# Block attention's TensorE steps: run after every 24 weight matmuls, two quarter tiles' worth together, instead of after every 12

## The chip, the cores and the metric

The kernel runs on one core of a Trainium2 chip. The metric is the device time of one execution in microseconds (us). TensorE (PE in the profile) does the matmuls, and the loading of its stationary operand is shown apart as PEld; VectorE is DVE, ScalarE is ACT, GpSimd is POOL, SyncE is SP.

## The reference, cut to what matters

One inference step of a two-layer decoder trunk, for a prompt of 256 tokens and 8 samples of 8 tokens (320 tokens in all, model width 2048, everything in float32). Layer 0 is a Mamba-2 / short-convolution mixer, layer 1 is block-sparse attention ("MoBA"); each is followed by a cross-attention into 256 memory tokens. The change touches layer 1 alone:

```
q, k, v, g = split(h @ w_in)                   # 2048 -> 5120 columns: 40 column tiles of 128
prompt:  s = q @ k.T + alibi; softmax; o = p @ v          # 16 heads, 4 KV heads, 256 tokens
sample:  kmean = mean of each 256-key block of the cache (8 blocks of 256 past keys, paged)
         the 3 blocks with the highest q . kmean are kept, and the own block of 8 new tokens
         s = q @ k_sel.T + alibi; softmax; o = p @ v_sel
out = (o * silu(g)) @ w_out                    # 2048 -> 2048: 16 column tiles
```

## The kernel before

All projections go through one stream of weight tiles of 2048x128 (1 MB each). SP loads tile n into one of 4 buffers (`Trunk.load`), ACT rounds it to float32r (`Trunk.high`, L123, 1.9 us), DVE makes the remainder (`Trunk.low`, L128, 2.3 us), and TensorE multiplies it in 48 matmuls of 128x320 (`Proj.parts`: 32 with the high half, L167, then 16 with the low half, L172). The results of successive tiles alternate between two banks of PSUM; DVE takes each one out (`evacuate`).

The attention is woven into the 40 tiles of the layer's input projection. Each tile is cut into 4 quarters of 12 weight matmuls (`weave`, L1670). Quarter qr = 4j + qi is quarter qi of tile j, and behind its 12 matmuls TensorE runs the attention steps that `Moba.steps(qr)` lists (L2169). The two loops of `scalar_program` and `vector_program` go over the same quarters in the same order, and do their halves of the same steps; all engines are tied by semaphores alone, each engine's queue strictly in order.

The samples are worked off in 8 units U (2 samples and 8 heads each), one unit per period of 12 quarters (3 tiles), starting at quarter 40. With x for the quarter inside a period (x = (qr - 40) mod 12), a period holds:

- **K** at x = 0, 3, 6, 9 (called K0 to K3 below): 16 transposes of key pages (L2315) into four fills of a ring of three PSUM banks. ACT copies each fill out to `past_keys` (L2424, x4), and a fill waits until the fill three before it in the ring has been copied (`turn_bank`, L2290).
- **S** at x = 2, 5, 8, 11: scores (L2334), with the own block at x = 11 (L2336). DVE takes them in (`scored`: L2607, L2608, L2611) and, for all but a few early ones, also waits for the T step of the same quarter.
- **T** at x = 5, 8, 11 and 2 of the next period: transposes of probabilities (L2343, L2345), one fill each, copied by ACT (L2430).
- **V** at x = 8, 11 and 2, 5 of the next: probabilities by values (L2358, L2366). **OT** at x = 8: the unit's result transposed (L2371), copied by ACT (L2440).
- DVE alone: `gather` at x = 1 (L2556, the queries that S at x = 2 needs), `biases` at x = 11 (L2573 to L2586), `inverse` at x = 8, `unit_out` at x = 7.
- ACT alone: `exps` of the unit before (L2457), 5 of them at x = 1 and 4 at x = 2, behind the copies of that quarter's steps; `high` at each third quarter (qi 3), behind the copies.

The prompt's heads run beside them, one per tile for tiles 11 to 18 and 23 to 30 (`head`): **pS** (L2381) at qi 0, then DVE's `prompt_scored` (L2640 to L2646), ACT's `prompt_exps` (L2465) at qi 1, DVE's `prompt_normed` at qi 2, and on the next tile **pT** (L2388, copied by L2447) at qi 0 and **pO** (L2396, L2397, copied by L2449) at qi 2. `rows` (L2306) transposes keys and values at qi 1 of 8 tiles. Inside a quarter the order is rows, OT, V, S, T, K, pT, pS, pO. On ACT `prompt_exps` stands ahead of the copies of its quarter:

```
2682                if qi == 1:
2685                    for h in self.head(j):
2686                        self.prompt_exps(act, h)
2689                for step in self.steps(qr):
2690                    self.scalar(act, step)
```

After the last period only T and V steps are left, and OT of unit 7 at quarter 156, the first of the last tile. What it yields goes through DVE's `samples_vector` (L2497), ACT's and DVE's `split` (L2510, L2521), and the output projection (`po.begin`, L197) waits for that.

Of the kernel before, what the change touches and what calls it, by code (L numbers as in the profile page):

```python
# [1669 lines left out]
def weave(pe, parts, steps, run):  # L1670

    for _ in range(12):
        next(parts, None)
    for step in steps:
        run(pe, step)


class Cross:
# [320 lines left out]
    def tensor_program(self, pe):  # L1999
        p, po, rin = self.p, self.po, self.rin  # L2000
        for j in range(8):
            parts = p.parts(pe, j, rin.rhs, rin.ready if j == 0 else None)
            for qi in range(4):
                weave(pe, parts, list(self.steps(4 * j + qi)), self.tensor)
            for _ in parts:
                pass
            if j == 0:
                rin.norm_tensor(pe)
        first = list(range(po.tps))
        pe.wait_ge(self.s["lo"], CAH)  # L2010
        po.begin(pe, first, list(range(CAH - 1)), self.rhs)
        pe.wait_ge(self.s["lo"], CAH + 1)
        po.end(pe, first, [CAH - 1], self.rhs)
        for t in range(po.tps, po.tiles):
            po.tile(pe, t, self.rhs)
# [84 lines left out]
class Moba:  # L2100
# [558 lines left out]
    def tensor_program(self, pe):  # L2659
        p, po, rin, n = self.p, self.po, self.rin, len(self.order)  # L2660
        for j in range(n):
            parts = p.parts(pe, j, rin.rhs, rin.ready if j == 0 else None)
            for qi in range(4):
                weave(pe, parts, list(self.steps(4 * j + qi)), self.tensor)
            for _ in parts:
                pass
            if j == 0:
                rin.norm_tensor(pe)
        early, late = list(range(self.TAIL)), list(range(self.TAIL, AH))
        pe.wait_ge(self.s["g_lo"], self.TAIL + 1)  # L2670
        po.begin(pe, [0], early, self.rhs)
        pe.wait_ge(self.s["g_lo"], AH + 1)
        po.end(pe, [0], late, self.rhs)
        for j in range(1, KC):
            po.tile(pe, j, self.rhs)
# [247 lines left out]
```

## Time and profile before

| | |
|---|---|
| median of 3 runs | 2048.36 us (2047.74 to 2052.03) |
| the profiled execution | 2050.37 us |
| its span in the trace | 2047.6 us |
| PE busy | 1996.8 us, 98% of the span |
| ACT, DVE, POOL busy | 46%, 57%, 10% |
| mean granted clock of TensorE | 0.992 of full speed |
| the stretch of the attention steps | about 1404 to 1796 us of the span |

Times in the trace count from the start of the span. PE rows show matmuls, PEld rows the weight loads that go just ahead of them; as every matmul here has its own load, the starts of PEld rows give TensorE's place in its program. A granted clock of 1.00 is 2.4 GHz, 0.50 is 1.2 GHz.

### The profile page before, as it was taken

Reading aid. Unit: us, or ns where it says so; the run is one execution under the profiler, and the core shown is the slowest. Engines: PE = TensorE matmul, PEld = TensorE weight load, DVE = VectorE, ACT = ScalarE, POOL = GpSimd, SP = SyncE. Lnnn points to the kernel's source line nnn. Section 1 sums busy time; section 2 is a strip of 40 time slices with the busy share of each in tenths; the row PEclk is TensorE's granted clock in tenths of the full one; section 3 lists DMA queues with packets and bytes.
Section 4 is the critical chain, followed back from the end, with each engine's and each line's share of the span. In section 5 each row is a group of like instructions: output and inputs, shape, how many; then the busy total and the mean of one; then the engine's idle time right before and its main releaser. Section 6 shows DMA issues by size and latency. Waiting matters only on the chain. (4 is left out here: it accounts for less than half of the span.)

```text
span 2047.6 us, 40019 instructions
## 1 busy us (share of the span) xinstructions
PE 1996.8 (98%) x15760; PEld 1912.6 (93%) x15760; DVE 1163.3 (57%) x1845; ACT 937.3 (46%) x1531; POOL 209.6 (10%) x363
## 2 busy tenths in 40 slices
PE   7999999999999999999999999899999999999996
PEld 6999999999999999999999999899888888999996
DVE  5647766657465574456545543644554655565446
ACT  7535455325344253254433335534565555443543
POOL 1001000010110101000100000020134333200000
PEclk8999999999999999999999999999999999999998
DMA  9487555565665656755555557386798988765741
GB/s 246 143 228 179 142 143 140 134 186 140 165 170 134 185 140 170 204 153 147 145 146 152 144 175 237 113 267 184 210 271 264 275 256 261 224 203 153 247 154 63
DMA packets 539549, 373.27 MB, mean 182 GB/s; under 512 B 14908, under 2 KB 509705, under 8 KB 538491
## 3 DMA queue, kind: packets, MB, share of 16 engines
q1 hardware_dynamic: 519666, 306.53, 53.7%
q0 software_dynamic: 19648, 64.18, 9.9%
q8 instruction: 125, 2.05, 0.4%
q14 instruction: 62, 0.50, 0.1%
q10 hardware_dynamic: 48, 0.02, 0.0%
HBM read 349.48 MB, written 21.19 MB: 181 GB/s over the span
## 5 line engine op out<-in xcount | busy, mean ns | idle before, releaser
L123 ACT ACTIVATE w_high<-w_raw 128x2048 fp32r<-128x2048 f32 x232 | 444.0, 1914 | 626.8 <-PE bank L172 546.9
L128 DVE TENSOR_TENSOR w_low<-w_raw,w_high 128x2048 fp32r<-128x2048 f32 x232 | 530.9, 2289 | 219.0 <-ACT w_high L123 218.8
L167 PE MATMUL bank<-x_hi,w_high 128*128 128x320 f32 x1664 | 494.2, 312 | 0.0
L167 PE MATMUL bank<-x_lo,w_high 128*128 128x320 f32 x1664 | 489.6, 309 | 0.0
L167 PEld LDWEIGHTS bank<-x_hi,w_high 128*128 128x128 f32 x1664 | 312.4, 188 | 1.0
L167 PEld LDWEIGHTS bank<-x_lo,w_high 128*128 128x128 f32 x1664 | 312.5, 188 | 0.6
L172 PE MATMUL bank<-x_hi,w_low 128*128 128x320 f32 x1664 | 260.9, 309 | 0.0
L172 PEld LDWEIGHTS bank<-x_hi,w_low 128*128 128x128 f32 x1664 | 248.3, 188 | 0.0
L167 PE MATMUL bank<-xo_x_hi,w_high 128*128 128x320 f32 x640 | 196.3, 320 | 1.9 <-issue 1.6
L167 PE MATMUL bank<-xo_x_lo,w_high 128*128 128x320 f32 x640 | 188.9, 309 | 0.0
L2230 POOL DMA_DIRECT2D value_pages<-in_cache_v x232 | 125.1, 539 | 210.0 <-issue 134.7
L167 PEld LDWEIGHTS bank<-xo_x_hi,w_high 128*128 128x128 f32 x640 | 120.2, 188 | 4.1 <-issue 2.8
L167 PEld LDWEIGHTS bank<-xo_x_lo,w_high 128*128 128x128 f32 x640 | 120.4, 188 | 0.5
L172 PE MATMUL bank<-xo_x_hi,w_low 128*128 128x320 f32 x640 | 106.2, 312 | 0.0
L172 PEld LDWEIGHTS bank<-xo_x_hi,w_low 128*128 128x128 f32 x640 | 95.6, 188 | 0.8 <-issue 0.8
L1410 DVE TENSOR_TENSOR xt<-xt,bank 128x320 f32<-128x320 f32 x80 | 38.7, 487 | 93.6 <-PE bank L172 93.6
L2424 ACT ACTIVATE past_keys<-bank 128x512 f32<-128x512 f32 x128 | 65.6, 597 | 30.3 <-PE bank L2315 30.3
L2607 DVE TENSOR_REDUCE ms_gate<-bank 128x2 f32<-128x512 f32 x32 | 22.1, 692 | 96.8 <-PE bank L2343 67.5
L167 PE MATMUL bank<-ysc_hi,w_high 128*128 128x320 f32 x256 | 76.3, 313 | 0.0
L167 PE MATMUL bank<-y_lo,w_high 128*128 128x320 f32 x256 | 75.3, 309 | 0.0
L167 PE MATMUL bank<-y_hi,w_high 128*128 128x320 f32 x256 | 75.3, 309 | 0.0
L167 PE MATMUL bank<-ysc_lo,w_high 128*128 128x320 f32 x256 | 75.3, 309 | 0.0
(451 smaller groups left out, 3451.3 us busy)
## 6 DMA issues: line engine op xcount, KB each, us to landing
w_raw<-in_ev_w_in SPq DMA_DIRECT2D x104, 1024.0 KB, 5.8
w_raw<-in_od_w_in SPq DMA_DIRECT2D x40, 1024.0 KB, 6.8
w_raw<-in_ev_w_out SPq DMA_DIRECT2D x32, 1024.0 KB, 6.0
key_pages<-in_cache_k SPq DMA_DIRECT2D x256, 128.0 KB, 3.0
value_pages<-in_cache_v POOLq DMA_DIRECT2D x232, 128.0 KB, 3.6
w_raw<-in_ca_w_kv SPq DMA_DIRECT2D x16, 1024.0 KB, 6.4
w_raw<-in_ca_w_q SPq DMA_DIRECT2D x16, 1024.0 KB, 5.8
w_raw<-in_od_w_out SPq DMA_DIRECT2D x16, 1024.0 KB, 6.0
```

Of the source, the lines that this page charges most:

```text
L123: self.nc.scalar.activation(self.w_high[n % HI][:], self.w_raw[n % RAW][:], ACT.Copy).then_inc(self.w_hi, 1)
L128: self.nc.vector.tensor_tensor(self.w_low[n % RAW][:], self.w_raw[n % RAW][:], self.w_high[n % HI][:].bitcast(F32), ALU.subtract).then_inc ...
L167: e.nc.tensor.matmul(out, hi[:, k, cols], rhs(k)[part], start=(k == 0 and part == 0), stop=False)
L172: m = e.nc.tensor.matmul(out, lo[:, k, cols], rhs(k)[0], start=False, stop=k == self.kch - 1)
L1410: e.nc.vector.tensor_tensor(e.xt[:, t, :], e.xt[:, t, :], p.bank(t)[:, 0:T], ALU.add).then_inc(e.bank_free, 1)
L2230: eng.dma_start(dst[c % 4][:, g:g + 1, :], src[ds(page, 1), :, 256 * hp:256 * hp + 256].rearrange("n t c -> t n c")).then_inc(sem, 16)
L2424: f(self.kt_past[:, 2 * bi + hi, :], b[:], ACT.Copy).then_inc(s["turn_out"], 1)
L2607: h.put(v.tensor_reduce(self.gate[:, 2 * a:2 * a + 2], b2(bank[:]), AX.X, ALU.add))
```

## The change

`Moba.tensor_program` alone is changed. The first 12 matmuls of each half tile are issued with no steps behind them, and the steps of both quarters, in their old order, come behind the next 12. The programs of ACT, DVE, SP and POOL, the number of instructions and every semaphore stay.

```diff
         for j in range(n):
             parts = p.parts(pe, j, rin.rhs, rin.ready if j == 0 else None)
-            for qi in range(4):
-                weave(pe, parts, list(self.steps(4 * j + qi)), self.tensor)
+            for half in range(2):
+                weave(pe, parts, [], self.tensor)
+                weave(pe, parts, [*self.steps(4 * j + 2 * half), *self.steps(4 * j + 2 * half + 1)], self.tensor)
             for _ in parts:
                 pass
```

So the quarters x = 0 and 1, 2 and 3, 4 and 5, 6 and 7, 8 and 9, 10 and 11 now share a place.

## Rows read from the trace of the kernel before

**Rows 1.** Windows: window, length, busy PE, PEld, DVE, ACT, POOL (instructions), clock, DMA share, GB/s.
```profile
1404.00:1796.00 392.00, 383.66 (x3688) 341.08 (x3687) 220.64 (x480) 218.11 (x497) 120.82 (x223) 1.00 0.83 247
```
**Rows 2.** Timeline of PEld, period 2, x = 3: start, length, what, count.
```profile
1494.89 1.77 PEld L172 LDWEIGHTS bank<-xo_x_hi,w_low 128*128 128x128 f32 x12
1496.62 1.89 PEld L2315 LDWEIGHTS bank<-const,key_pages 128*128 128x128 f32 x16
```
**Rows 3.** Timeline of PEld, period 2, x = 8 and 9.
```profile
1514.72 0.24 PEld L2334 LDWEIGHTS bank<-past_keys,ms_q 128*32 128x32 f32 x8
...
1516.52 0.53 PEld L2381 LDWEIGHTS bank<-m_k,m_q 128*128 128x128 f32 x4
1518.90 1.38 PEld L2315 LDWEIGHTS bank<-const,key_pages 128*128 128x128 f32 x12
1521.48 0.42 PEld L2315 LDWEIGHTS bank<-const,key_pages 128*128 128x128 f32 x4 [1.20 <-ACT past_keys L2424]
```
**Rows 4.** Timeline of DVE and ACT, the same stretch.
```profile
1516.57 0.69 DVE L2607 TENSOR_REDUCE ms_gate<-bank 128x2 f32<-128x512 f32 x1 [3.63 <-PE bank L2343]
...
1519.51 0.41 DVE L2646 TENSOR_REDUCE mp_negmax<-mp_p 128x1 f32<-128x256 f32 x1
...
1519.96 0.41 ACT L2465 ACTIVATE mp_p<-mp_p,mp_negmax 128x128 f32<-128x128 f32 x1 [2.48 <-DVE mp_negmax L2646]
...
1520.85 2.04 ACT L2424 ACTIVATE past_keys<-bank 128x512 f32<-128x512 f32 x4
```
**Rows 5.** Waits, 1404 to 1796 us: who waited for whom, us, times, longest.
```profile
PEld bank L2315 <- ACT past_keys L2424: 5.1, 5, 1.2
...
PEld bank L2334 <- DVE ms_q L2556: 3.9, 6, 1.3
...
PE bank L2315 <- ACT m_vrows L2417: 2.0, 2, 1.1
```
**Rows 6.** Timeline of PEld and ACT, period 3, x = 2 and 3.
```profile
1538.98 0.41 PEld L2397 LDWEIGHTS bank<-mp_pt,m_vrows 128*128 128x128 f32 x2
...
1539.89 0.50 ACT L2457 ACTIVATE ms_p<-ms_p,ms_bias 128x256 f32<-128x256 f32 x1
...
1541.02 1.90 PEld L2315 LDWEIGHTS bank<-const,key_pages 128*128 128x128 f32 x16
...
1541.87 2.03 ACT L2424 ACTIVATE past_keys<-bank 128x512 f32<-128x512 f32 x4
```
**Rows 7.** Timeline, the last tile of the projection and the start of the next.
```profile
1790.68 0.14 PEld L2371 LDWEIGHTS bank<-const,ms_orows 128*128 128x128 f32 x1
...
1791.88 1.09 DVE L2497 SCALAR_TENSOR_TENSOR m_q<-m_q,m_sample_gate 128x896 f32<-128x896 f32 x1
...
1795.48 1.09 DVE L2521 TENSOR_TENSOR m_o_lo<-m_q,m_o_hi 128x896 fp32r<-128x896 f32 x1
...
1796.62 0.19 PEld L197 LDWEIGHTS bank<-m_o_hi,w_high 128*128 128x128 f32 x1 [0.50 <-DVE m_o_lo L2521]
```
**Rows 8.** Timeline of PE, idle stretches elsewhere.
```profile
30.64 0.98 PE L270 MATMUL bank<-const,x_rows 128*128 128x128 f32 x3 [2.70 <-ACT vb L281]
...
46.88 2.31 PE L270 MATMUL bank<-const,x_rows 128*128 128x128 f32 x12
50.64 0.66 PE L270 MATMUL bank<-const,kv_turned 128*128 128x128 f32 x2 [1.45 <-ACT xt L281]
...
1208.66 0.61 PE L167 MATMUL bank<-evy_x_hi,w_high 128*128 128x320 f32 x1 [3.83 <-PEq L105]
```
**Rows 9.** Windows about them, columns as in rows 1.
```profile
30.20:36.90 6.70, 6.26 (x28) 5.81 (x29) 6.04 (x3) 5.89 (x7) 0.00 (x0) 0.50 1.14 279
...
50.70:54.00 3.30, 3.30 (x16) 3.30 (x17) 3.19 (x5) 2.00 (x5) 0.00 (x0) 0.50 0.49 122
...
1208.70:1214.40 5.70, 5.70 (x22) 5.70 (x22) 3.21 (x2) 1.76 (x1) 0.00 (x0) 0.50 0.98 337
2034.00:2040.50 6.50, 3.88 (x34) 3.38 (x32) 5.91 (x12) 2.98 (x5) 0.00 (x0) 1.00 0.33 99
```

## The prediction

> **What bounds the kernel now.** I read the page first: TensorE is busy for 98% of the span. Then the windows: in the 392 us of the attention steps it is busy for 383.7 us at the full clock, ACT and DVE for 56% each [rows 1]. So TensorE's order of work sets the time, and its few waits are the only slack. The change removes no instruction, so it can act through two things: waits and the clock.
>
> Next the timeline of the weight loads, which shows TensorE's place. A burst of 12 weight matmuls takes 1.73 us (1494.89 to 1496.62), a K step of 16 transposes 1.9 us [rows 2]. The burst of 12 is a cover: for 1.73 us TensorE works while ACT and DVE digest the step before. The change takes that cover away between an even quarter and the odd one behind it, and doubles it ahead of the even one. Work whose producer and consumer are two quarters apart has 24 matmuls between before and after, so K to S, pT to pO and gather to S are as covered as they were. The question is which odd quarter needs something from the even one. The ring of three banks gives the answer: a K step makes four fills, so its last fill must wait until ACT has copied its first. Wherever ACT has other work queued between the even quarter's copies and the first K copy, TensorE now stands. K0 and K2 come first in their pairs; K1 (x = 3) and K3 (x = 9) are second.
>
> **Part 1: K3 behind a prompt head, 6 times (tiles 12, 15, 18, 24, 27, 30).** ACT's queue at x = 9 has `prompt_exps` ahead of the K copies, and it waits for DVE. The scores of S end up in DVE, behind T, at 1516.57; three operations on them and four of `prompt_scored` end at 1519.9; `prompt_exps` starts at 1519.96 and the first K copy at 1520.85 [rows 4]. TensorE has issued pS by 1517.06, has its 12 weight matmuls until 1518.90, makes 12 transposes until 1520.28, waits 1.20 us and issues the last four at 1521.48 [rows 3]. Counted from pS's end, the release comes at +4.42 us. This chain starts with S and T, holds no weight matmul and stays. After the change TensorE needs +1.38 us to reach the wait, so it waits 3.04 us, 1.8 more. The pair ends at about +4.87 against +4.84 before, and 12 weight matmuls (1.76 us at 0.147 us each) that lay inside it are now executed ahead of it: net 1.8 us. The waits view has today's ones: 5 on the K copy, 2 on `m_vrows`, where a rows step sits in between [rows 5]. 6 x 1.8 = 10.8 us.
>
> **Part 2: K1 behind the exponentials, 7 times (periods 1 to 7).** At x = 2 ACT copies T and pO, then does four `exps`, and only then K1's copies. pO's loads are issued by about 1539.3; the exponentials run from 1539.89 to 1541.87, where the first K copy starts [rows 6]; it takes 0.6 us, so the fourth fill may start at 1542.5, or +3.2. Today the weights cover that: K1 starts at 1541.02 and runs 1.90 us without a wait [rows 6]. After, the fourth fill is reached at +1.38 and stands 1.8 us; the pair ends at +3.65 where it ended at +3.6, and the 12 matmuls are extra: 1.8 us net. 7 x 1.8 = 12.6 us. Period 0 has no `exps`, and the last ones no K.
>
> **Part 3: K3 without a head (twice)** needs only T's copy first: which starts 0.3 us behind T and takes 0.6, so the fourth fill is late by some 0.15 us (an estimate from the copies' 0.6 us; bounds 0 and 0.6): 0.3 us.
>
> **Part 4: the end.** OT of unit 7 is alone at quarter 156, an even one, so it is issued 1.76 us later. Today: OT at 1790.68, `samples_vector` 1791.88, the last `split` 1795.48, and the next projection starts at 1796.62 after a wait of 0.50 us [rows 7]. Of the shift all or nearly all comes through, as `samples_vector` starts 1.2 us behind OT today, of which other work of DVE may hold a part: between 1.2 and 1.76 us; I take +1.6 us.
>
> **Part 5: what is gained.** The second cover is now doubled: between T and own scores at x = 11 and S at x = 2 lie 48 weight matmuls where 36 lay. DVE's `biases` and `gather` sit there, and the waits for `ms_q` are 3.9 us in 6 [rows 5]; they go, for about -3 us (the bounds: 0 and -3.9).  A merged boundary between weights and steps may save or cost up to 0.2 us; some 20 are merged where no wait hides it, so from -4 to +4 us; I take 0, since the one that I can compare, 12 matmuls between pO and K1 at 1.73 us [rows 2] against 1.76 for 12 without a boundary, shows 0.03.
>
> SP's and POOL's queues: page loads wait for K or V of two Qs (6 quarters) earlier. K0 and K2 move back by 1.76 us relative to the weights, their consumers are 6 quarters, some 20 us, further on; no wait for a page shows among TensorE's waits. `high` and `low` are a tile ahead, and the tile's last matmul keeps its place. Cost 0.
>
> Sum without the clock: 10.8 + 12.6 + 0.3 + 1.6 - 3 = +22.3 us.
>
> **Part 6: the clock.** Idle time of 3.04 us among transposes is new here. What the rows show of such stretches: after 2.70 us idle among transposes the clock was 0.50 for the next 6.7 us; after 12 transposes, 1.45 us idle and 2 more, 0.50 for 3.3 us; after 3.83 us idle between weight matmuls 0.50 until 1214.4 [rows 8, 9]. Today's 1.0 to 1.2 us in the K3 steps leave it at 1.00 [rows 1]. Nearest to 3.04 is 2.70, so a drop is likely, though it won't fall at each of the six. At the low clock 22 weight matmuls took 5.70 us, 0.26 each instead of 0.147 [rows 9]: 0.11 x 22 = 2.5 us for one drop. Bounds: none, and 13 drops (every K3 and K1) with 33 us. I take 3 drops of the six K3 waits, none at K1 (1.8 us idle between 12 and 4 transposes): +7.5 us, for **+29 us** and a bit in all.
>
> Do transposes hold the clock? At the end of the kernel TensorE does little but transposes from 2034 to 2040.5, 3.88 us of 6.5 busy, and the clock stays at 1.00 [rows 9]; the stretch at 46.9 fell. The Trainium skill ("TensorE: Matmul & The Clock Gate", Part 4: PE-mode transpose) says that transposes don't count as PE activity for the clock. By that rule the K steps are as good as idle time, so K3 (4.9 us) would drop nearly always and K1 (3.7 us) often. The trace agrees at 46.9 and speaks against it at 2034.
>
> The sum is against the profiled execution, 2050.4, and would give 2080 there; the median of the runs is 2.0 us lower, so I forecast **2077 us** (+1.4%).
>
> **The rivals.**
> - *Stalls only, the clock holds* (0.30): parts 1 to 5 as they are, at most one drop. For: the idle time is broken by transposes, and 2034 held. Against: 2.70 and 1.45 us fell. 2048.4 + 22.3 = 2071, or 2066 to 2075 with the bounds of part 5.
> - *The forecast* (0.48): 2 to 5 drops, 2074 to 2084.
> - *Transposes don't hold the clock* (0.14): all six K3 and some 4 of the K1 stretches: 22.3 + 10 x 2.5 = +47, 2096.
> - *Faster* (0.03): the waits move without costing. The mechanism would be ACT: if `prompt_exps` and `exps` were through before TensorE reaches the fourth fill, parts 1 and 2 vanish and only the gains stay, -3 for `ms_q` and up to -4 at the boundaries, against +1.6 for the end: about -5, 2043. It decides at +1.38 us behind the even quarter's last step; the rows put the release at +4.42 and +3.2, so it needs DVE's chain to be half as long.
> - *No change* (0.05): the stalls are real but the doubled cover elsewhere gives them back, since waits of other steps that I missed hold TensorE today. Only 11 to 12 us of named waits exist in the whole stretch, so at the most half. 2048.
>
> What a measurement here can tell from no change is about 0.2%, 4 us. Chances: faster 0.03, same 0.05, slower 0.92. The range for 8 in 10: from the stall case's lower end, 2065, to the case of six drops and unfavourable boundaries, 2090.
>
> **What would show it.** In the profile after, the waits view must have L2315 <- ACT past_keys at about 30 us in some 13 waits, the longest 3.0 us; K3's last four transposes stay 4.4 us behind pS and K1's 3.2 us behind pO. The wait of L2334 for `ms_q` must be gone, and that of L197 for L2521 must read about 2.1 us. Windows behind the K3 steps must show a clock below 1.00 for three or so of the six. ACT's and DVE's busy times stay. If the K3 waits are far below 3 us, the chain through DVE isn't what I think; if clock stays 1.00 everywhere, part 6 falls and the time is 2071; if TensorE waits elsewhere (V, S for a page, L167 for `w_high`), the cost of the moved queues was wrong.

## The result and the profile after

| | before | after |
|---|---|---|
| median us | 2048.51 (2047.74 to 2052.03, 4 runs) | 2078.24 (2077.06 to 2081.21, 4 runs) |
| ratio | | 1.0144, 95% interval 1.0126 to 1.0161 |
| span of the profiled execution | 2047.6 | 2075.1 |
| mean granted clock | 0.992 | 0.988 |

The change costs 29.7 us, 1.4%. The page's head and busy times of the changed kernel:

```profile
span 2075.1 us, 40019 instructions
PE 2000.9 (96%) x15760; PEld 1917.3 (92%) x15760; DVE 1162.0 (56%) x1845; ACT 937.0 (45%) x1531; POOL 209.0 (10%) x363
```

The work is the same: as many instructions, ACT and DVE as busy as before. Most of the 27.5 us by which the span grew are time in which TensorE stands still; some 6 us, as run 5 will show, are time in which it runs slowly. All of it lies in the attention's stretch. From the first rows step (L2306) to the first weight load of the output projection (L197) the kernel before takes 1796.62 - 1341.85 = 454.8 us, the changed one 1823.98 - 1341.06 = 482.9, 28.1 more; what comes behind is 251.0 us before and 251.1 after. This *stretch* is the better measure for the parts below, since what comes ahead of it differs from one execution to the next: over the ten traces the first rows step starts between 1339.5 and 1345.7 us. The stretch ends with the one wait of part 4:

```profile
1823.98 0.19 PEld L197 LDWEIGHTS bank<-m_o_hi,w_high 128*128 128x128 f32 x1 [1.91 <-DVE m_o_lo L2521]
```

TensorE's waits in the changed kernel (waits view, 1404 to 1824 us; engine and line that waited, releaser, us in total, times, longest):

```profile
PEld bank L2315 <- ACT past_keys L2424: 24.9, 11, 3.0
...
PEld bank L2315 <- issue: 6.8, 3, 3.1
...
PE bank L2315 <- ACT m_vrows L2417: 5.5, 2, 2.9
...
PEld bank L197 <- DVE m_o_lo L2521: 1.9, 1, 1.9
...
PE bank L2358 <- issue: 1.4, 1, 1.4
...
PEld bank L2334 <- DVE ms_q L2556: 0.4, 1, 0.4
```

Against [rows 5]: the waits for the K copy went from 5.1 us in 5 to 24.9 in 11, those behind a rows step from 2.0 to 5.5, and the wait for `ms_q` from 3.9 to 0.4. The PEld and the PE row of a line are mostly the same waits, seen at the weight load and at the matmul. The 11 of the first row are the seven K1 waits (1.84 us, once 1.96) and four of the K3 waits (2.96 us). The other two K3 waits, in tiles 12 and 24, stand behind a rows step, which takes a fill of the ring itself, so there it is the third K fill that waits; their weight loads, 2.89 and 3.08 us, are in the "issue" row. All in all TensorE waits 30.8 us in 13 places, where the prediction said about 30 in some 13.

The timeline of the weight loads at x = 8 and 9 of period 2, the place of [rows 3], shows one of the K3 waits:

```profile
1525.06 0.53 PEld L2381 LDWEIGHTS bank<-m_k,m_q 128*128 128x128 f32 x4
1525.62 1.45 PEld L2315 LDWEIGHTS bank<-const,key_pages 128*128 128x128 f32 x12
1530.03 0.42 PEld L2315 LDWEIGHTS bank<-const,key_pages 128*128 128x128 f32 x4 [2.96 <-ACT past_keys L2424]
```

pS ends at 1525.6, and the last four transposes start 4.4 us later, as they did before; but the 12 weight matmuls that lay in these 4.4 us now come ahead of pS. ACT's and DVE's rows there are the ones of [rows 4] in unchanged order:

```profile
1528.07 0.41 DVE L2646 TENSOR_REDUCE mp_negmax<-mp_p 128x1 f32<-128x256 f32 x1
...
1528.51 0.40 ACT L2465 ACTIVATE mp_p<-mp_p,mp_negmax 128x128 f32<-128x128 f32 x1 [2.48 <-DVE mp_negmax L2646]
...
1529.40 2.03 ACT L2424 ACTIVATE past_keys<-bank 128x512 f32<-128x512 f32 x4
```

And x = 2 and 3 of period 2, the place of [rows 6] one period earlier:

```profile
1501.35 0.41 PEld L2397 LDWEIGHTS bank<-mp_pt,m_vrows 128*128 128x128 f32 x2
1501.68 1.34 PEld L2315 LDWEIGHTS bank<-const,key_pages 128*128 128x128 f32 x12
1504.86 0.42 PEld L2315 LDWEIGHTS bank<-const,key_pages 128*128 128x128 f32 x4 [1.84 <-ACT past_keys L2424]
```

Windows of the changed kernel (columns as in rows 1): the attention steps as a whole, then behind five of the six K3 steps with a head. Four are at half clock, with 13 to 15 matmuls in 3 us where about 20 fit at the full one (0.147 us each); the last has no drop. The sixth, in tile 12, has none either.

```profile
1404.00:1824.00 420.00, 389.07 (x3684) 346.76 (x3682) 219.62 (x481) 218.52 (x497) 120.44 (x223) 0.98 0.78 231
...
1480.30:1483.20 2.90, 2.90 (x13) 2.90 (x13) 1.01 (x4) 1.25 (x3) 1.39 (x3) 0.50 1.11 339
...
1531.20:1534.40 3.20, 3.20 (x14) 3.20 (x13) 0.14 (x1) 0.23 (x1) 1.07 (x2) 0.50 1.03 330
1620.00:1623.20 3.20, 3.20 (x15) 3.20 (x14) 0.55 (x2) 1.20 (x3) 1.13 (x3) 0.50 1.13 317
1671.20:1674.40 3.20, 3.20 (x14) 3.20 (x14) 0.00 (x0) 0.33 (x1) 0.81 (x2) 0.50 1.07 347
1720.20:1723.50 3.30, 3.30 (x25) 3.30 (x24) 0.87 (x4) 1.36 (x4) 1.51 (x3) 1.00 1.10 329
```

### The profile page after: what moved, and what is told of

It is laid out like the page before. It is cut to its first block and busy times, and to the rows that moved or that the text cites. A ratio compares the mean times of both kernels' runs of the same rounds, so it can differ in the third digit from the quotient of the medians.

```text
span 2075.1 us, 40019 instructions
## 1 busy us (share of the span) xinstructions
PE 2000.9 (96%) x15760; PEld 1917.3 (92%) x15760; DVE 1162.0 (56%) x1845; ACT 937.0 (45%) x1531; POOL 209.0 (10%) x363
## 5 line engine op out<-in xcount | busy, mean ns | idle before, releaser
L2315 PE MATMUL bank<-const,key_pages 128*128 128x128 f32 x512 | 65.6, 277 | 27.8 <-ACT past_keys L2424 22.2
L2315 PEld LDWEIGHTS bank<-const,key_pages 128*128 128x128 f32 x512 | 57.4, 141 | 33.4 <-ACT past_keys L2424 24.9
```

The costliest lines, as they stand in the source:

```text
L2315: t = nc.tensor.transpose(bank[:, 128 * g:128 * g + 128], self.kring[c % 4][:, g, 128 * hi:128 * hi + 128], e.ident)
```

## The experiments

**1. Merge x = 2 and 3 alone; 2. merge x = 8 and 9 alone.** The diff to the kernel before; the second has `(8,)` for `(2,)`.

```diff
-            for qi in range(4):
-                weave(pe, parts, list(self.steps(4 * j + qi)), self.tensor)
+            for half in range(2):
+                qr = 4 * j + 2 * half
+                if (qr - self.BASE0) % self.PERIOD in (2,):
+                    weave(pe, parts, [], self.tensor)
+                    weave(pe, parts, [*self.steps(qr), *self.steps(qr + 1)], self.tensor)
+                else:
+                    weave(pe, parts, list(self.steps(qr)), self.tensor)
+                    weave(pe, parts, list(self.steps(qr + 1)), self.tensor)
```

> Only the quarters x = 2 and 3 share a place; all others are as before. My theory (the ring's fourth K fill waits for ACT's copy behind the exponentials): 7 waits of 1.8 us at K1, net 7 x 1.8 = +12.6 us, less the waits for ms_q, 3 us, since S at x = 2 now has 36 weight matmuls behind pS where 24 lay: 2058 us, clock at 1.00 throughout. Rival (merging costs by itself, per merged boundary, and not by the K copies): 8 merged places of the 40 or so of the full change, a fifth of its 29.7 us, +6 us: 2054 us. Rival (the losses are clock drops above all): with no K3 wait made longer nothing drops: 2048 to 2051 us.

> Only the quarters x = 8 and 9 share a place, the one at OT of unit 7 (quarters 156 and 157) among them. My theory: six K3 waits of 3.0 us for 1.2, net 10.8 us; about 4 clock drops of 1.5 us behind them, 6 us; the end 1.6 us: +18 us, 2067 us, with the waits for ms_q as before (3.9 us in 6). Rival (merging costs by itself): 2054 us. Rival (transposes, not idle time, drop the clock): drops behind K1 or K0 too.

Measured: 2058.68 us (ratio 1.0046, 1.0033 to 1.006) and 2068.08 us (1.0096, 1.008 to 1.0111); the kernel before on that chip 2048.76. The stretch takes 463.8 us and 473.4, 9.1 and 18.7 more than before. First the waits (1404 us to the end of the stretch) of the one with x = 2 and 3, then its clock:

```profile
PEld bank L2315 <- ACT past_keys L2424: 17.8, 11, 2.0
```
```profile
1404.00:1807.00 403.00, 385.46 (x3698) 342.92 (x3696) 222.07 (x482) 218.03 (x497) 120.82 (x223) 1.00 0.81 241
```

It has the seven K1 waits beside the old K3 ones, no row for `ms_q` any more, and the full clock, and its time is 0.7 us above my 2058. The one with x = 8 and 9 keeps `ms_q` as it was, waits up to 3.0 us at K3, has the longer wait at the end, and shows half clock in four windows:

```profile
PEld bank L2315 <- ACT past_keys L2424: 12.2, 5, 3.0
...
PEld bank L2334 <- DVE ms_q L2556: 3.8, 6, 1.3
...
PEld bank L197 <- DVE m_o_lo L2521: 1.9, 1, 1.9
```
```profile
1478.60:1481.60 3.00, 3.00 (x13) 2.82 (x12) 0.00 (x0) 0.04 (x1) 0.91 (x2) 0.50 1.03 334
1526.30:1529.30 3.00, 3.00 (x14) 3.00 (x13) 0.94 (x4) 1.19 (x3) 1.55 (x3) 0.50 1.07 349
1611.70:1614.70 3.00, 2.66 (x12) 2.69 (x13) 1.56 (x4) 2.35 (x6) 1.23 (x3) 0.50 1.19 319
1710.70:1713.70 3.00, 3.00 (x12) 2.81 (x12) 0.00 (x0) 0.28 (x2) 0.92 (x2) 0.50 0.90 301
```

The run came out 1 us above my 2067. Its four drops are not all at the places of the changed kernel. In tile 27, where the changed kernel had one (at 1671.2), TensorE waits just as long here and keeps the full clock; in tile 30 it is the other way round:

```profile
1661.02 0.42 PEld L2315 LDWEIGHTS bank<-const,key_pages 128*128 128x128 f32 x4 [2.96 <-ACT past_keys L2424]
```
```profile
1660.90:1664.20 3.30, 3.18 (x22) 3.13 (x23) 1.39 (x4) 1.97 (x6) 1.62 (x3) 1.00 1.07 335
```

The two parts make 27.8 us of the stretch's 28.1, so the other four pairs of quarters add up to 0.3 (a wait of 1.4 us for a value page at x = 5 among it, of which more below). A price per merged boundary, the same everywhere, is ruled out: ten merged places at x = 2 (not the eight that I had counted) cost 9.1 us, ten at x = 8 cost 18.7, and the other four pairs together 0.3.

**3. The change with ACT's copies first.** All of the change stays; only ACT's order is another.

```diff
             for qi in range(4):
                 qr = 4 * j + qi
+                if qi == 0 and j == 1:
+                    rin.norm_scalar(act)
+                if qr == 48:
+                    act.wait_ge(self.s["spilled"], 16)
+                if qi % 2 == 0:
+                    for step in [*self.steps(qr), *self.steps(qr + 1)]:
+                        self.scalar(act, step)
                 if qi == 1:
-                    if j == 1:
-                        rin.norm_scalar(act)
                     for h in self.head(j):
                         self.prompt_exps(act, h)
-                if qr == 48:
-                    act.wait_ge(self.s["spilled"], 16)
-                for step in self.steps(qr):
-                    self.scalar(act, step)
```

> The changed kernel, but ACT runs the copies of both quarters of a half ahead of prompt_exps and exps. My theory: the fourth fill of K1 and K3 waits 0 to 0.2 us, the clock stays at 1.00 in the whole stretch; of the 29.7 us nothing stays but the end (1.6 us) and the value page (1.4 us), and 1.1 us at each of six K3 and 3 us for ms_q are gained against before: 2048.5 - 6.6 - 3 + 3 = 2042 us. Rival (merging costs by itself, or the copies are late for another reason): above 2055 us. Rival (transposes drop the clock): drops stay, some 6 us: 2048 us.

Measured: 2046.17 us (ratio to before 0.9986, 0.9977 to 0.9995), with runs from 2040.63 to 2048.52; the profiled run took 2041.55. In it the stretch is 447.8 us, 35.1 less than with the change alone and 6.9 less than before, and no wait for a K copy is left in the waits view. The K3 step of period 2, with pS ahead of it, and the clock:

```profile
1514.24 0.53 PEld L2381 LDWEIGHTS bank<-m_k,m_q 128*128 128x128 f32 x4
1514.79 1.92 PEld L2315 LDWEIGHTS bank<-const,key_pages 128*128 128x128 f32 x16
```
```profile
1404.00:1785.00 381.00, 378.65 (x3670) 338.61 (x3669) 215.29 (x472) 216.37 (x495) 120.88 (x223) 1.00 0.84 251
```

That is the cause shown directly: with the merged steps kept and only the queue of ACT turned round, the whole loss goes. The profiled run is where I put it (2042 us); the median is 4 us above, and run 8 bears on why.

**4. Transposes without idle time.** The kernel before with every K transpose issued three times:

```diff
-                for g in range(4):
+                for g in [0, 1, 2, 3] * 3:
                     t = nc.tensor.transpose(bank[:, 128 * g:128 * g + 128], self.kring[c % 4][:, g, 128 * hi:128 * hi + 128], e.ident)
```

> The kernel before, with every K transpose issued three times in a row (the two extra ones write the same data to the same place): 32 stretches of about 5.5 us that hold transposes alone and no idle time. If idle time is what drops the clock: it stays at 1.00, 32 x 2 x 1.82 us = +116 us less the K3 waits that are covered, 2158 to 2165 us. If transposes don't count as activity: a drop behind nearly each of the 32, 1.5 us or more each, another +48 us or more: above 2205 us.

Measured: 2147.62 us (ratio 1.048, two runs). A K step is now 5.3 us of transposes alone (timeline), and the clock over the whole stretch (windows) stays full:

```profile
1509.12 5.31 PEld L2315 LDWEIGHTS bank<-const,key_pages 128*128 128x128 f32 x48
```
```profile
1400.00:1890.00 490.00, 489.87 (x4710) 453.61 (x4709) 218.74 (x473) 226.64 (x495) 120.41 (x223) 1.00 0.67 195
```

32 such stretches and no drop: transposes hold the clock, so it isn't they that drop it in the changed kernel; run 5 tests the idle time. The time is 10 us under the lower end that I gave: a K step grew by 3.45 us (5.31 for 1.86), not by 3.64, for 110 us, and the waits at K3 (7 us) and for `ms_q` (3 us) went under it.

**5. The stall kept, its idle time filled.** The changed kernel; in the six K3 steps behind a head the fill that comes last before the wait repeats its transposes.

```diff
+                late = (0, 1) if Q // 4 in (0, 4) else (1, 0)
+                again = 7 if Q % 4 == 3 and Q // 4 not in (3, 7) and (bi, hi) == late else 1
-                for g in range(4):
+                for g in [0, 1, 2, 3] * again:
```

> The changed kernel, but in the six K3 steps behind a prompt head the fill ahead of the waiting one repeats its four transposes seven times (24 more, 2.7 us, same data to the same place), so that TensorE is busy while it would wait. The wait for ACT is as long, only not idle. My theory (idle time drops the clock, the stall itself is ACT's chain): the time of the stall stays, the clock stays at 1.00 in the whole stretch, the four drops of the changed kernel go: 2078.2 - 6 = 2072 us. Rival (long stretches without weight matmuls drop it, idle or not): 4 or more drops stay, 2078 us. Rival (the drops cost next to nothing since ACT's work catches up): 2078 us at a clock of 1.00.

Measured: 2070.75 us, against 2078.24 for the change alone (with 2049.72 for before in its own series: ratio 1.0099, 1.0084 to 1.0114, where the change has 1.0144, 1.0126 to 1.0161, so the intervals lie apart). The timeline at K3 of period 2 and the windows over the stretch:

```profile
1528.81 4.07 PEld L2317 LDWEIGHTS bank<-const,key_pages 128*128 128x128 f32 x36
1533.22 0.42 PEld L2317 LDWEIGHTS bank<-const,key_pages 128*128 128x128 f32 x4 [0.35 <-ACT past_keys L2426]
```
```profile
1404.00:1821.00 417.00, 403.23 (x3859) 360.94 (x3857) 221.70 (x482) 218.28 (x497) 120.47 (x223) 1.00 0.79 233
```

The K3 step is as long as in the changed kernel, the clock is full, and the stretch is 475.4 us, 7.5 less. Of these, 1.4 us are the wait of L2358 near the end, which this trace doesn't have; the other 6.1 us I put down to the four drops, 1.5 us each. So idle time at this wait drops the clock, and the same wait filled with transposes doesn't.

**6 and 7. The kernel before with copies first, and with `gather` ahead of `low` too.**

```diff
                 if qi == 1 and j == 1:
                     rin.norm_scalar(act)
...
                 for step in self.steps(qr):
                     self.scalar(act, step)
+                if qi == 1:
+                    for h in self.head(j):
+                        self.prompt_exps(act, h)
```
```diff
-                if qi == 1 and j:
-                    e.low(dve, m + j - 1 + AHEAD)
                 for U in self.rel(qr, 1):
                     self.gather(dve, U)
+                if qi == 1 and j:
+                    e.low(dve, m + j - 1 + AHEAD)
```

> The kernel before, but ACT runs the copies of a quarter ahead of prompt_exps. My theory: the waits of 1.0 to 1.2 us at six K3 steps go, the waits for ms_q stay: 2048.7 - 6.6 = 2042 us. Rival (a shorter stretch runs into the page loads, which SP issues at about 1.2 us each, 8 per K step): some of it is lost, with TensorE waiting for key_pages or value_pages: 2044 to 2048 us, with a wide spread.

> As the run before, and DVE runs gather ahead of the weights' low half at x = 1, so that S at x = 2 has its queries 2.3 us earlier. My theory: the waits for ms_q go too, 3.2 us: 2039 us. Rival (page loads): no faster than the run before, since every us gained is given back as waits for pages.

Measured: 2043.39 us (ratio 0.9967, 0.9954 to 0.998) and 2041.43 us (0.9959, 0.9943 to 0.9974), before 2049.72. The stretch is 447.7 and 444.9 us, 7.1 and 9.8 less than before: the waits that [rows 5] show, taken away one after the other. Both medians lie above what I expected, by 1.4 us (2042) and 2.4 us (2039). Each is faster than the kernel before by its interval; between the two of them the intervals overlap, so that `gather` gains anything is shown by the traces alone. The second's runs spread from 2036.6 to 2047.6, so page loads may cost it something in some of them; its one trace has no such wait.

**8. The third once more, for a second trace.**

> The same kernel as e3, whose runs spread from 2040.6 to 2048.5 us, once more for a second trace. My theory: the clock is at 1.00 in the stretch each time, and a slower run shows TensorE waiting for pages (L2315 for key_pages, L2358) for the difference. Rival: a slower run shows clock drops.

Measured: 2046.85 us (2041.06 to 2054.96), the profiled run 2048.37. Its stretch is 453.9 us, 6.0 more than in the first trace of the same kernel. The waits (1320 to 1830 us), TensorE's place, the clock behind it and SP's queue:

```profile
PEld bank L2315 <- DMA key_pages<-in_cache_k: 5.9, 3, 3.4
```
```profile
1603.07 1.50 PEld L2315 LDWEIGHTS bank<-const,key_pages 128*128 128x128 f32 x8 [3.42 <-DMA key_pages<-in_cache_k]
```
```profile
1603.00:1607.00 4.00, 3.93 (x18) 3.93 (x19) 0.82 (x4) 2.07 (x6) 1.60 (x3) 0.57 0.79 231
```
```profile
1565.17 9.58 SPq L2230 DMA_DIRECT2D key_pages<-in_cache_k  x8
1574.80 0.94 SPq L116 DMA_DIRECT2D w_raw<-in_od_w_in  x1
1576.50 9.73 SPq L2230 DMA_DIRECT2D key_pages<-in_cache_k  x8
1586.28 0.79 SPq L116 DMA_DIRECT2D w_raw<-in_od_w_in  x1
1587.84 20.96 SPq L2230 DMA_DIRECT2D key_pages<-in_cache_k  x16
```

TensorE stood 3.4 us for a key page and got half clock behind it, so my theory and its rival had a part each: the page waits come first, and one of them brings a drop. SP issues pages nearly without a break from 1565 to 1608, 1.2 to 1.3 us each. With the copies out of the way, the next thing that holds the stretch is the key pages, in some executions more than in others. The page that the 3.4 us were spent on is the eighth of that step. Here and in the trace of run 3, DMA views of the one load (us from issue to landing at the end):

```profile
key_pages<-in_cache_k SPq DMA_DIRECT2D x1, 128.0 KB, 4.6
```
```profile
key_pages<-in_cache_k SPq DMA_DIRECT2D x1, 128.0 KB, 2.4
```

SP issued it at 1598.43 here and at 1595.20 there, so it came 3.2 us later and took 2.2 us longer to land. Both SP's queue and the transfer have a share, and which of them would have to be mended was not tested.

## Why the prediction was right

The forecast was 2077 us, 2065 to 2090; measured 2078.24. The terms of the prediction add up to +29.8 us, which is 2078 on the median and not 2077. By its own parts, the stretch's growth read from the starts of the weight loads:

| part | forecast us | measured us |
|---|---|---|
| 1. K3, six waits | 10.8 | 10.6 |
| 2. K1, seven waits | 12.6 | 12.3 |
| 3. K3 without a head | 0.3 | 0 |
| 4. the end | 1.6 | 1.4 (wait of 1.91 for 0.50) |
| 5. `ms_q` | -3 | -3 |
| 6. clock | 7.5 (3 drops of 2.5) | 6.1 (4 drops of 1.5) |
| not foreseen: wait of V for a page | 0 | 1.4 |
| K0 behind `high` (1.94 us in six periods before, 1.85 after) | not counted | -0.5 |
| sum | 29.8 | 28.3 (the stretch itself: 28.1) |

*Parts 1 and 2* held in size and mechanism. The release of the fourth fill came 4.4 us behind pS, as forecast, since no weight matmul lies in that chain; TensorE's wait was 2.96 us for a forecast of 3.04, and 1.84 for 1.8 at K1. Runs 1 and 2 give each part alone, run 3 removes both by ACT's order. One reading was off: of the five waits on the K copy in [rows 5] four are K3's; the fifth, 0.31 us, is the K1 of period 4. That K1 grew by 1.65 us instead of 1.8, a matter of 0.15 us in the sum. The condition that the rival *faster* had named, ACT's copies through before TensorE reaches the last fill, is what run 3 sets up, and there the loss is gone.

*Part 5*, boundaries taken as 0: right. From the last load of pS to the first of V it takes 0.52 us and to a weight load 0.22, 0.3 more; from one weight load to V it took 0.38 us and to another weight load 0.147, 0.23 more. So what a merged boundary costs is about what the old one did. The other four pairs came to 0.3 us in all.

*Part 6* was right in kind and off in both factors. 4 of 6 K3 waits dropped the clock and no K1 wait did, but a drop cost 1.5 us and not 2.5. I had sized it by the one behind 3.83 us of idle time, which held for 22 matmuls [rows 9]; here TensorE had half clock for only some 14. That 7.5 and 6.1 lie so close is luck: one drop too few, each too dear. Which of the waits drop the clock isn't fixed by their length: 2.96 us of idle time dropped it in some places and not in others, and in tiles 27 and 30 the changed kernel and run 2 differ. What decides is open.

The rival that transposes don't hold the clock falls: the windows row of run 4 reads 1.00 over 490 us. By the Trainium skill's sentence ("TensorE: Matmul & The Clock Gate", Part 4: PE-mode transpose), that transposes don't count as PE activity, there would have been drops at nearly every one of the 32 K steps. For these float32 transposes the measurement decides against it.

*The queues* that I set to 0 were not wholly free. The V step of unit 7 at quarter 153 waited 1.4 us in the changed kernel and not before. POOL issued the last value pages late there, at 1800.5 and 1803.8 for a step due at 1808.6, with 1.5 and 2.7 us between issues where 0.6 is usual. The DMA view of the last one reads 6.3 us from issue to landing:

```profile
value_pages<-in_cache_v POOLq DMA_DIRECT2D x1, 128.0 KB, 6.3
```

1803.8 + 6.3 = 1810.1, and V starts at 1810.15, so this page is what it waited for. In the kernel before, the last page from POOL was issued behind a gap of 2.6 us too, but landed in 4.4 us, ahead of its V step. Why the landing took longer stays open.

## What to carry to other kernels

When work is gathered into larger bursts on the engine that sets the time, look at each pair that becomes adjacent and ask what the second needs from the first through another engine; the instructions that stand in that engine's queue between the two copies are then exposed, however idle the engine is on average. Here a ring of three banks and four fills in a step made one such need per step, and the cure was not the spacing but the order on the consuming engine: copies that free a bank go ahead of long work that waits for a third engine. And a wait of about 3 us is dearer than it looks, since TensorE may come out of it at half clock: here 4 of 6 did, at 1.5 us each.

## What the runs showed of the hardware

- Idle time among transposes dropped TensorE's clock, transposes by themselves didn't: 2.9 to 3.1 us idle did so in 4 of 6 places in the changed kernel and in 4 of 6 in run 2, partly others; 3.4 us did in run 8; 1.84 us did in none of 7, 5.3 us of transposes in none of 32. The length of one wait isn't all: in the kernel's opening 1.45 us idle was enough, where 12 transposes ahead of it took 2.31 us [rows 8, 9] and not 1.4 as in a K step.
- A drop behind a wait of 3 us lasted about 3.4 us (in run 8, 4.00 us at a mean clock of 0.57) and cost 1.5 us; the one behind 3.83 us held for 5.7 us at least [rows 9].
- Key pages of 128 KB leave SP's queue one per 1.2 to 1.3 us when issued without a break, which is close to what this stretch consumes: 8 and a weight tile now and then per K step, of which run 8 starts one in about 10.5 us (31 intervals from 1405.3 to 1731.7).
